# Recurrent chain ranked ahead, spatial maps loaded in the first block, pooling map folded into a weight, pool states by transposes

## The chip, the cores and the metric

One Trainium2 chip, all 8 cores of it; each core runs the same program on its own data, and nothing passes between them. The metric is the device time of one execution, in microseconds, of the slowest core.

## What is computed

Two layers of a hybrid decoder over 8 prompt sequences of 2048 tokens and 128 sample sequences of 8 tokens, width 1024. The reference, cut:

```python
hn = rms_norm(h, norm_mix)
q, k, v, g_out, g_lr, xp, u, vv, gates = split(hn @ w_in)
# A: gated linear attention, 4 heads, d_k 128, d_v 256
g_log = log_sigmoid(g_lr @ w_gk2 + b_gk) / 16
o, s_new = gla_mix(q, k, v, g_log, s_gla)       # S_t = diag(a_t) S_{t-1} + k_t^T v_t, o_t = q_t S_t
branch_a = (rms_norm(o, gla_norm) * silu(g_out)) @ w_br_a
# B: pooling, windows 2/4/8/16, one 128x128 map for each of 4 channel groups
pooled = means - xp
pool_out = einsum('ntgc,gcd->ntgd', pooled, w_mix) * scale
branch_b = pool_out @ w_br_b                    # state: the last 15 rows of [history, xp]
# C: spatial gating in chunks of 128
branch_c = (gelu(u) * (tril(w_s) gelu(vv) + b_s)) @ w_br_c
merged = ga * branch_a + gb * branch_b + gc * branch_c     # ga, gb, gc = sigmoid(gates)
h = h + merged @ w_out
h = h + relu(rms_norm(h, norm_ffn) @ w_ff1)**2 @ w_ff2
```

The outputs are the tokens after a last norm, and the new states of A, B and C. The recurrence starts from zero for a prompt and from a given state (32 pieces of 256 KB a core and layer) for the samples.

## The kernel before

Each core takes one prompt sequence and 16 sample sequences: 17 tiles of 128 tokens, tile 0 being the 16 x 8 sample tokens. The tiles make 5 blocks of 3, 3, 3, 4 and 4 tiles (`BLK`, L24). A product in bf16 covers a block, so its free size is 384 or 512 columns. The normed input of all blocks (`hn`) stays in SBUF for a whole layer.

The main loop (L1100 to L1149) runs, for each layer: the recurrent stage over 5 blocks; the mixing stage over 5 blocks; the gate stage, two halves of the output width over 5 blocks each; the output projection; the feed-forward layers.

*Recurrent stage.* `gla_project` (L744) makes q, k, v and the decays, `gla_gate` (L809) the output gate, `gla_scan` (L838) walks over the prompt tiles with a state `U` and its bf16 copy `Sb` per head. In the scan each tile takes transposes of the keys (`kq` to `ktok`), masked scores (`attT`), the output product, the update of the state on DVE and its copy on ScalarE, and the norm of the output (`o_norm`, L821) with Ln and Exp on ScalarE, where `gla_gate` uses Silu: different function sets of ScalarE, each swap being an ACT_TABLE_LOAD.

*Sample states.* `gla_sample` (L883) is a generator of 32 steps, 8 of which are recorded with each block. A step loads one state into one of five buffers `Sf` (SP's queue), casts it on POOL into one of two `Sinb` (L404), has TensorE multiply the queries with it (`kqS`, `Sinb`) and form the update (`km`, `vS`), updates `Sf` on DVE and writes it out (`gla_s`). The steps are numbered 0 to 31 here; step n uses buffer n mod 5, so its load waits for the write-out of step n - 5.

*Mixing stage.* `mix_block` (L932) projects xp, pools it on DVE into the first half of a block's `OBC`, multiplies each of its 4 channel groups with the pooling map `wpm` and evicts it on ScalarE with the scale, projects u and vv, and applies the spatial map `wsT` (the samples' `wsS`) with the bias. For the new pooling states it projects xp once more, tokens by channels, for the sample tile and the last tile (`proj_tm`). `OBC` is written to HBM and read back in the gate stage as `OBs`; the output of branch A goes the same way as `H4s`.

*Maps.* `mix_prep` (L685) stands after the recurrent stage: it loads the spatial maps in fp32 (`wsp`) on SP's queue and masks them on DVE into `wsT`; an 8 x 8 corner (`w8`) is spread over the 16 samples by a product on TensorE (`rep`).

*Weights.* A ring of 7 slots (`wring`), 2 MB in fp32 each, cast to bf16 on the way, loaded on POOL's queue in a fixed order: v0 v1 k q g0 g1 xp u vv, then for each half ga ba gb bbc gc, and so on (L599 to L616). The slot `bbc` holds half of `w_br_b` and half of `w_br_c`. A load is issued by POOL once the readers of its slot's old content are done.

*What sets the order.* Nothing runs in the order of the code. Every instruction is recorded as a node with a cost (`record`, L199), and `schedule` (L245) places the nodes: per engine it takes the ready node with the least pair of start time and key. The key is the node's number in the code, plus 60 for a node of ScalarE that needs another function set. PSUM tiles are given 8 banks in the same pass. All products are issued at L421, all transposes at L434.

The core of one sample step (L906 to L909):

```python
s = Sf[n % 5]
spq.dma(s.t[:, :, :], sgla[l, i, 2 * hp:2 * hp + 2].rearrange("h d e -> d h e"), writes=[s])
sb_ = Sinb[n % 2]
vcopy(sb_.t[:, :, :], s.t[:, :, :], [s], [sb_], E=POOL)
```

Of the kernel before, what the change touches and what calls it, by code (L numbers as in the profile page):

```python
# [141 lines left out]
class Node:
    __slots__ = ("E", "fn", "reads", "writes", "late", "occ", "lat", "aset", "idx", "succ", "need", "ready", "tiles", "byts")


def build_program():
# [98 lines left out]
    def schedule():  # L245
        free = {id(E): 0.0 for E in (PE, ACT, DVE, SP, POOL)}
        ready = {id(E): [] for E in (PE, ACT, DVE, SP, POOL)}
        bank_at = [0.0] * 8
        bank_of = [None] * 8
        waiting = [n for n in nodes if n.E is PE and any(b.lw is not None for b in n.tiles)]  # L250
        opened = set()
        tiles_in_order = []
# [6 lines left out]
        oldest = 0  # L259
        aset = None  # L260
        dma_at = {id(SP): 0.0, id(POOL): 0.0}
        for n in nodes:
            if n.need == 0:
                ready[id(n.E)].append(n)
        left = len(nodes)
        while left:
            while oldest < len(tiles_in_order) and id(tiles_in_order[oldest]) in opened:
                oldest += 1
            best = None
            for E in (PE, ACT, DVE, SP, POOL):  # L270
                f = free[id(E)]
                pick = None
                for n in ready[id(E)]:
                    s = n.ready if n.ready > f else f
                    key = n.idx
                    bk = None
                    if E is PE and n.tiles and n.tiles[0].k is None:
                        b = n.tiles[0]
                        can = [k for k in b.allowed if bank_of[k] is None]
                        if not can or (len(can) < 2 and b is not tiles_in_order[oldest]):  # L280
                            continue
                        bk = min(can, key=lambda k: bank_at[k])
                        if bank_at[bk] > s:
                            s = bank_at[bk]
                    if E is ACT and n.aset is not None and n.aset != aset:
                        key += 60
                    c = (max(s, f + 30.0), key)
                    if pick is None or c < pick[0]:
                        pick = (c, s, n, bk)
                if pick is not None and (best is None or pick[1] < best[1]):  # L290
                    best = pick
            assert best is not None, "no node can be placed"
            _, s, n, bk = best
            E = n.E
            occ = n.occ
            if E is ACT and n.aset is not None and n.aset != aset:
                occ += 1300.0
                aset = n.aset
            ready[id(E)].remove(n)
            free[id(E)] = s + occ  # L300
            fin = s + occ + n.lat
            if n.byts:
                at0 = max(dma_at[id(E)], s + occ)
                other = dma_at[id(POOL if E is SP else SP)]
                work = n.byts / (310.0 if E is SP else 233.0)
                both = max(0.0, other - at0)
                dma_at[id(E)] = at0 + (both + work - both / 2 if work > both / 2 else work * 2)
                fin = dma_at[id(E)] + 2500.0
            for b in n.tiles:
                if b.k is None:  # L310
                    b.k = bk
                    bank_of[bk] = b
                    opened.add(id(b))
                b.left -= 1
                b.last = max(b.last, fin)
                if b.left == 0:
                    bank_of[b.k] = None
                    bank_at[b.k] = b.last
            rs, ws, lt = real(n.reads), real(n.writes), real(n.late)
            n.fn(rs, ws, lt)  # L320
            for m in n.succ:
                t = fin + (60.0 if m.E is not E or E is not PE else -n.lat)
                if t > m.ready:
                    m.ready = t
                m.need -= 1
                if m.need == 0:
                    ready[id(m.E)].append(m)
            left -= 1
        return max(free.values())
# [132 lines left out]
    r8 = sbc("r8_t", [8, 128])  # L462
# [216 lines left out]
    def mix_consts(l):  # L679
        plq.dma(wpm.t[:, :, :], w_pm[l].rearrange("g c d -> c g d"), writes=[wpm])  # L680
# [251 lines left out]
    def mix_block(l, b):  # L932
# [42 lines left out]
        if b == 0 or b == NB - 1:  # L975
            ps = proj_tm(s, view, b, 0 if b == 0 else nt - 1)
            act(xptok.t[:, :], ps.t[:, :], AF.Copy, [ps], [xptok])
            if b == 0:
                spq.dma(pool_s[l][:, 7:15, :], xptok.t[:, :], reads=[xptok])
            else:  # L980
                spq.dma(pool_p[l], xptok.t[113:128, :], reads=[xptok])
# [236 lines left out]
```

How the kernel before makes its waits and increments, by code:

```python
    def wait(self, tok):  # L41
        if tok is None:
            return
        sem, val = tok
        if sem is self.sem and self.name == "pe":
            return
        k = id(sem)
        if self.seen.get(k, 0) >= val:
            return
        self.e.wait_ge(sem, val)
        self.seen[k] = val
# [1 line left out]
    def tok(self, inst):  # L53
        self.cnt += 1
        inst.then_inc(self.sem, 1)
        return (self.sem, self.cnt)
# [282 lines left out]
            def fn(rs, ws, lt):  # L339
                k = self.i % len(self.sems)
                self.i += 1
                sem = self.sems[k]
                if self.cnt[k] > 0:
                    self.E.wait((sem, 16 * self.cnt[k]))
                acquire(self.E, rs, ws)
                for b in after:
                    self.E.wait(b.w)
                self.E.e.dma_start(out=out, in_=in_).then_inc(sem, 16)
                self.cnt[k] += 1
                release((sem, 16 * self.cnt[k]), rs, ws)
# [283 lines left out]
        def fn(rs, ws, lt):  # L634
            acquire(POOL, rs, ws)
            for view, src in todo:
                nc.gpsimd.dma_start(out=view, in_=src).then_inc(slot_sem[k], 16)
                slot_cnt[k] += 1
            release((slot_sem[k], 16 * slot_cnt[k]), rs, ws)
```

## Time and profile before

| | |
|---|---|
| runs | 3 |
| median | 2469.94 us |
| lowest | 2469.77 us |
| the profiled execution | 2468.97 us |
| its span (core 3, the slowest; the others from 2456.0) | 2467.9 us |
| TensorE (PE) busy | 2379.9 us, 96% of the span |
| VectorE (DVE) busy | 1280.2 us, 52% |
| ScalarE (ACT) busy | 874.9 us, 35% |
| GpSimd (POOL) busy | 125.8 us, 5% |

The profile is of one execution on its slowest core. A busy time is the time in which the engine has an instruction under way; a matmul's end is modelled, and matmuls overlap. PEclk is the clock that was granted to TensorE, as a part of full speed. "x <- y" in a wait says that the instruction which writes x stood still until y was done, and a name such as `OBC` stands for all its buffers. The layers show as two like stretches: the recurrent stage of layer 0 ends near 300 us, that of layer 1 near 1510 us.

### The profile page before, as it was taken

What the parts mean: (1) busy time and instruction counts of PE and PEld (TensorE: products, weight loads), DVE (VectorE), ACT (ScalarE), POOL (GpSimd) and SP (SyncE); (2) the same over time, 40 slices, a digit from 0 to 9 for tenths busy, and PEclk for the clock granted to TensorE, in tenths of its full rate; (3) what the DMA queues carried; (4) which work ended last, traced back from release to release, by engine and by line L of the source; (5) the groups of instructions that cost most, each with busy time, mean ns of one, the idle gap of its engine ahead of it and who ended that gap; (6) DMA issues with size and microseconds to landing.
All of it is one profiled execution on the core that took longest, in us unless ns stands there. A gap on an engine that the chain in (4) does not pass through costs nothing.

```text
span 2467.9 us, 40917 instructions; the slowest of 8 cores (2456.0 to 2467.9 us)
## 1 busy us (share of the span) xinstructions
PE 2379.9 (96%) x13590; PEld 1248.0 (51%) x13590; DVE 1280.2 (52%) x2258; ACT 874.9 (35%) x1803; POOL 125.8 (5%) x179
## 2 busy tenths in 40 slices
PE   6899889999999999999999997999999999999998
PEld 3554445645545444545555554555464454545453
DVE  4776575434456444434656666744343754444455
ACT  4975454222223111212346566532222322111133
POOL 2011100000000000000000110000000000000000
PEclk9999899999999999999999998999999999999999
DMA  9534955236183040405171356562632621322112
GB/s 170 151 92 97 186 174 126 72 69 128 71 169 52 1 69 1 69 1 105 80 133 39 125 96 129 177 129 82 108 94 78 130 50 19 51 35 35 18 61 86
DMA packets 176387, 219.45 MB, mean 89 GB/s; under 512 B 12562, under 2 KB 160538, under 8 KB 173080
## 3 DMA queue, kind: packets, MB, share of 16 engines
q0 software_dynamic: 81168, 78.23, 22.9%
q1 hardware_dynamic: 95016, 138.62, 17.5%
q8 instruction: 115, 1.88, 0.3%
q14 instruction: 88, 0.72, 0.1%
HBM read 240.45 MB, written 55.05 MB: 120 GB/s over the span
## 4 chain that ended last, share of the span: by engine, by line
PE 88%; DVE 3%; DMA 3%; issue 3%; ACT 3%; SPq 0%; POOL 0%; DVEq 0%; ACTq 0%; POOLq 0%
PE ps L421 87%; DMA Sf<-sgla 2%; PE ps L434 1%; DMA wring<-w_in 1%; DVE tmp L395 1%; ACT L384 1%; DMA gla_s<-Sf 0%; ACT rsg L384 0%; DVE Sf L395 0%; ACT Sb L384 0%; ACT sqg L384 0%; DVE xn L395 0%; DVE go L392 0%; DVE U L395 0%; SPq L348 0%
## 5 line engine op out<-in xcount | busy, mean ns | idle before, releaser
L421 PE MATMUL ps<-hn,wring 128*128 128x384 bf16 (+1 forms) x6400 | 1247.0, 348 | 3.1 <-ACT ssq L384 1.1
L421 PEld LDWEIGHTS ps<-hn,wring 128*128 128x128 bf16 x6400 | 624.6, 98 | 545.6 <-issue 9.7
L421 PE MATMUL ps<-wring,a 128*128 128x512 bf16 x2176 | 477.5, 379 | 0.2 <-DVE a L392 0.2
L384 ACT ACTIVATE rl<-ps 128x384 f32<-128x384 f32 (+1 forms) x320 | 170.4, 533 | 644.5 <-PE ps L421 536.3
L392 DVE TENSOR_TENSOR h<-h,ps 128x512 f32<-128x512 f32 x340 | 233.1, 687 | 258.0 <-PE ps L421 255.5
L421 PEld LDWEIGHTS ps<-wring,a 128*128 128x128 bf16 x2176 | 212.5, 98 | 253.2 <-issue 0.7
L392 DVE TENSOR_TENSOR a<-rl 128x384 bf16<-128x384 f32 (+1 forms) x320 | 195.4, 611 | 277.2 <-ACT rl L384 272.0
L384 ACT ACTIVATE sg<-ps 128x384 f32<-128x384 f32 (+1 forms) x240 | 128.0, 533 | 453.7 <-PE ps L421 323.2
L421 PE MATMUL ps<-wring,hn 128*128 128x512 bf16 x848 | 199.8, 384 | 11.5 <-DMA wring<-w_in 8.1
L392 DVE TENSOR_TENSOR tmp<-sg,ps 128x384 f32<-128x384 f32 (+1 forms) x160 | 97.2, 608 | 155.5 <-ACT sg L384 79.8
L421 PE MATMUL ps<-OBs,wring 128*128 128x384 bf16 (+1 forms) x640 | 143.8, 347 | 0.0
L392 DVE TENSOR_TENSOR acc<-sg,ps 128x384 f32<-128x384 f32 (+1 forms) x80 | 48.6, 608 | 173.1 <-PE ps L421 173.1
L421 PEld LDWEIGHTS ps<-wring,hn 128*128 128x128 bf16 x848 | 82.1, 99 | 103.7 <-issue 19.7
L421 PE MATMUL ps<-H4s,wring 128*128 128x384 bf16 (+1 forms) x640 | 130.7, 347 | 0.0
L421 PE MATMUL ps<-wring,mg 128*128 128x512 bf16 x544 | 120.7, 379 | 0.0
L421 PEld LDWEIGHTS ps<-H4s,wring 128*128 128x128 bf16 x640 | 62.6, 98 | 55.0
L421 PEld LDWEIGHTS ps<-OBs,wring 128*128 128x128 bf16 x640 | 62.6, 98 | 55.0
L421 PEld LDWEIGHTS ps<-wring,mg 128*128 128x128 bf16 x544 | 52.5, 98 | 60.0
L637 POOL DMA_DIRECT2D wring<-w_ff x32 | 28.0, 875 | 1063.7 <-PE ps L421 1062.0
L395 DVE SCALAR_TENSOR_TENSOR tmp<-ps,vec_t,rsg 128x256 f32<-128x256 f32 x136 | 63.8, 479 | 30.7 <-ACT rsg L384 27.7
L384 ACT ACT_TABLE_LOAD x51 | 65.4, 1283 | 37.4 <-PE ps L421 30.4
L395 DVE SCALAR_TENSOR_TENSOR Sf<-Sf,eblS,ps 128x256 f32<-128x256 f32 x128 | 58.4, 475 | 20.2 <-PE ps L421 19.4
(137 smaller groups left out, 1788.4 us busy)
## 6 DMA issues: line engine op xcount, KB each, us to landing
wring<-w_ff POOLq DMA_DIRECT2D x32, 1024.0 KB, 14.2
wring<-w_in POOLq DMA_DIRECT2D x30, 1024.0 KB, 15.9
Sf<-sgla SPq DMA_DIRECT2D x64, 256.0 KB, 4.2
gla_s<-Sf SPq DMA_DIRECT2D x64, 256.0 KB, 4.0
H4s<-H_d SPq DMA_DIRECT2D x12, 768.0 KB, 6.7
OBs<-OB_d SPq DMA_DIRECT2D x12, 768.0 KB, 6.2
h_d<-h SPq DMA_DIRECT2D x17, 512.0 KB, 2.6
h<-h_d SPq DMA_DIRECT2D x17, 512.0 KB, 8.1
```

What stands on the lines that cost most here:

```text
L384: op(ACT, lambda: nc.scalar.activation(out=now(out), in_=now(in_), func=func, **kw), reads, writes, occ, 125.0, SETS.get(func))
L392: op(E, lambda: E.e.tensor_tensor(out=now(out), in0=now(in0), in1=now(in1), op=alu), reads, writes, occ, 90.0)
L395: op(DVE, lambda: nc.vector.scalar_tensor_tensor(out=now(out), in0=now(in0), scalar=scalar, in1=now(in1), op0=op0, op1=op1), reads, writes ...
L421: inst = nc.tensor.matmul(now(m[0]), m[1], m[2], start=m[3], stop=m[4], **kw)
L434: inst = nc.tensor.transpose(now(o), i, ident_ap)
L637: nc.gpsimd.dma_start(out=view, in_=src).then_inc(slot_sem[k], 16)
```

## The change

Four edits. The first is in the scheduler: it is written anew as `lay_out(seed)`, and `schedule` takes the best of `ORDERS` layouts, of which there is one. A node's key is now its `rank`, its number less `lift`; `lift` is 200 while `gla_scan` is recorded, 0 elsewhere. A node of ScalarE that needs another function set has 400 ns added to its start in the comparison, besides the 60 on its key. The bookkeeping of nodes, banks and DMA times is otherwise the same.

The second: `mix_prep` and (in layer 0) `mix_consts` are recorded in block 0 of the recurrent stage. The spatial maps are loaded on POOL's queue in bf16 directly into `wsT` and masked in place, and the spread corner `rep` comes from the host; both loads have to follow the load of slot 6 of the ring.

The third: the pooling map is transposed on the host, scaled on DVE, and multiplied into the `w_br_b` half of slot `bbc` at the first block of each half of the gate stage: 4 products of 512 columns, evicted on ScalarE into the slot itself. The products with the pooling map in `mix_block` and their evictions are gone, so `OBC` holds the pooled values.

The fourth: the pooling states come from 4 fp32 transposes of channels already there (`xptok` for the samples, `phist` for the prompt), and the two projections of xp for them are gone.

```diff
@@ constants
+ORDERS = 1
+LIFT = 200
@@ record, lay_out, schedule
+        n.rank = n.idx - lift[0]
...
+        key_of = [n.rank + a for n, a in zip(nodes, (rng.random(len(nodes)) * 4.0 * (seed > 0)).tolist())]
+        swap = 400.0 if seed == 0 else float(rng.integers(0, 1300))
...
+                    c0 = max(s, f + 30.0)
+                    key = key_of[n.idx]
+                    if e == 1 and n.aset is not None and n.aset != aset:
                         key += 60
-                    c = (max(s, f + 30.0), key)
+                        c0 += swap
+                    c = (c0, key)
@@ mix_consts, mix_prep
-        plq.dma(wpm.t[:, :, :], w_pm[l].rearrange("g c d -> c g d"), writes=[wpm])
+        plq.dma(wpm.t[:, :, :], w_pmT[l].rearrange("g d c -> d g c"), writes=[wpm])
+        for g in range(4):
+            ts(wpm.t[:, g, :], wpm.t[:, g, :], vec_t.t[:, V_PSC + l * 4 + g:V_PSC + l * 4 + g + 1], ALU.mult, [wpm, vec_t], [wpm])
...
-        spq.dma(wsp.t[:, :, :], w_spT[l].rearrange("g s t -> s g t"), writes=[wsp], after=[hnB[NTILE - 1]])
-        spq.dma(w8.t[:, :, :], w_spT[l][:, 0:8, 0:8].rearrange("g s t -> s g t"), writes=[w8], after=[hnB[NTILE - 1]])
-        tt(wsT.t[:, :, :], wsp.t[:, :, :], cm.t[:, 0, :].unsqueeze(1).broadcast_to([128, 4, 128]), ALU.mult, [wsp, cm], [wsT])
-        ps = psum()
-        pe_group([(ps.t[:, 0:32], r8.t[:, :], w8.t[:, :, :].rearrange("s g t -> s (g t)"), True, True)], [r8, w8], [ps])
-        act(rep.t[:, :], ps.t[:, 0:32], AF.Copy, [ps], [rep])
+        plq.dma(wsT.t[:, :, :], w_spT[l].rearrange("g s t -> s g t"), writes=[wsT], after=[slots[6]])
+        spq.dma(rep.t[:, :], rep_d[l], writes=[rep], after=[slots[6]])
+        tt(wsT.t[:, :, :], wsT.t[:, :, :], cm.t[:, 0, :].unsqueeze(1).broadcast_to([128, 4, 128]), ALU.mult, [wsT, cm], [wsT])
@@ mix_block
+                act(xptok.t[:, g * 128:(g + 1) * 128], ps.t[:, 0:128], AF.Copy, [ps], [xptok])
...
-        if b == 0 or b == NB - 1:
-            ps = proj_tm(s, view, b, 0 if b == 0 else nt - 1)
+        if b == 0:
+            ps = psum()
+            pe_transposes([(ps.t[:, g * 128:(g + 1) * 128], xptok.t[:, g * 128:(g + 1) * 128]) for g in range(4)], ident.t[:, :], [xptok, ident], [ps])
             act(xptok.t[:, :], ps.t[:, :], AF.Copy, [ps], [xptok])
...
+        if b == NB - 1:
+            ps = psum()
+            pe_transposes([(ps.t[0:15, g * 128:(g + 1) * 128], phist.t[:, g, :]) for g in range(4)], ident.t[:, :], [phist, ident], [ps])
...
-        for g in range(4):
-            ps = psum()
-            pe_group([(ps.t[:, 0:T], wpm.t[:, g, :], ob[:, g, 0:T], True, True)], [wpm, poolB[par][g]], [ps])
-            act(ob[:, g, 0:T], ps.t[:, 0:T], AF.Copy, [ps, vec_t], [poolB[par][g]], scale=vec_t.t[:, V_PSC + l * 4 + g:V_PSC + l * 4 + g + 1])
@@ gate_block
+        if b == 0:
+            for g in range(4):
+                ps = psum()
+                pe_group([(ps.t[:, :], wpm.t[:, g, :], bbc[1][:, g, :], True, True)], [wpm, bbc[0]], [ps])
+                act(bbc[1][:, g, :], ps.t[:, :], AF.Copy, [ps], [bbc[0]])
@@ main loop
+            lift[0] = LIFT
             gla_scan(l, b)
+            lift[0] = 0
             if b == 0:
+                if l == 0:
+                    mix_consts(l)
+                mix_prep(l)
                 samples = gla_sample(l)
...
-        if l == 0:
-            mix_consts(l)
-        mix_prep(l)
```

**Order of TensorE.** The end of layer 0's recurrent stage on TensorE, before. `hn,wring` are products of a projection; `kqS,Sinb` uses a sample state (113 and 114 are the two cast buffers; the first row is step 20, the other one 21); `km` is a state's update; `kq`, `ktok`, `v` and `attT` belong to the scan of the last block, `hst` to the pooling history.

```order
L421 MATMUL ps<-kqS,Sinb_113 128x8 x4
L421 MATMUL ps<-hn,wring 128x512 x8
L421 MATMUL ps<-vS,km_117 128x256 x2
L421 MATMUL ps<-hn,wring 128x512 x64
L421 MATMUL ps<-kqS,Sinb_114 128x8 x4
L421 MATMUL ps<-vS,km_118 128x256 x2
L434 MATMUL ps<-ident_bf,kq_73 128x128 x4
L421 MATMUL ps<-kq_73 128x128 x4
L421 MATMUL ps<-w,r_t 128x32
L434 MATMUL ps<-ident_t,hst 128x120 x4
L434 MATMUL ps<-ident_bf,kq_73 128x128 x4
```

The same place after, from the group behind step 20's product to the one that step 22 follows:

```order
L452 MATMUL ps<-hn,wring 128x512 x8
L452 MATMUL ps<-vS,km_117 128x256 x2
L452 MATMUL ps<-glr,wgk_bf 128x512
L452 MATMUL ps<-hn,wring 128x512 x16
L452 MATMUL ps<-glr,wgk_bf 128x512
L452 MATMUL ps<-hn,wring 128x512 x32
L465 MATMUL ps<-ident_bf,kq_73 128x128 x12
L452 MATMUL ps<-hn,wring 128x512 x8
L452 MATMUL ps<-kq_73 128x128 x4
L452 MATMUL ps<-v_75,ktok_102 128x256 x2
L452 MATMUL ps<-kqS,Sinb_114 128x8 x4
L452 MATMUL ps<-v_75,ktok_102 128x256 x2
```

Between the products of steps 20 and 21 there are 72 projection products before and 64 after, and after them the scan's first transposes and scores stand ahead of step 21 too, with the update of step 20 further forward.

**Order of POOL.** POOL in the same stretch, before: casts of states 17 to 21 (`Sinb<-Sf`), and the issues of weight loads (`wring`: u and vv, then ga0, ba0, gb0) and of layer 1's small gate weights (`wglr`, `wgk`).

```order
L404 CAST Sinb_114<-Sf_110 128x512
L348 DMA wglr<-w_in 128x8x16
L637 DMA wring<-w_in 128x8x512 x2
L404 CAST Sinb_113<-Sf_111 128x512
L404 CAST Sinb_114<-Sf_112 128x512
L348 DMA wgk_bf<-w_gk 16x512 x4
L404 CAST Sinb_113<-Sf_108 128x512
L637 DMA wring<-w_in 128x8x512
L637 DMA wring<-w_br_a 128x8x512
L637 DMA wring<-w_in 128x8x512
L404 CAST Sinb_114<-Sf_109 128x512
L637 DMA wring<-w_br_b 128x4x512
```

After, from the cast of state 18 on; the row ahead of these is the issue of the u weights, and the first `wring` row in it is the issue of the vv weights, then come ga0, ba0 and gb0.

```order
L435 CAST Sinb_113<-Sf_111 128x512
L435 CAST Sinb_114<-Sf_112 128x512
L665 DMA wring<-w_in 128x8x512
L435 CAST Sinb_113<-Sf_108 128x512
L379 DMA wgk_bf<-w_gk 16x512 x4
L665 DMA wring<-w_in 128x8x512
L665 DMA wring<-w_br_a 128x8x512
L435 CAST Sinb_114<-Sf_109 128x512
L435 CAST Sinb_113<-Sf_110 128x512
L435 CAST Sinb_114<-Sf_111 128x512
L435 CAST Sinb_113<-Sf_112 128x512
L665 DMA wring<-w_in 128x8x512
```

The issue of vv has moved from ahead of states 18 and 19 to behind them, and that of gb0, here the last row, from ahead of state 21 to behind state 24.

**Order of TensorE, second place.** Layer 0's gate stage, where the second half begins: `OBs` products are those of the first half's last block, `H4s` products those of the second half's first. Before:

```order
L421 MATMUL ps<-hn,wring 128x512 x8
L421 MATMUL ps<-OBs_131,wring 128x512 x4
L421 MATMUL ps<-hn,wring 128x512 x8
L421 MATMUL ps<-OBs_131,wring 128x512 x4
L421 MATMUL ps<-hn,wring 128x384 x8
L421 MATMUL ps<-H4s_130,wring 128x384 x8
L421 MATMUL ps<-hn,wring 128x384 x8
L421 MATMUL ps<-H4s_130,wring 128x384 x8
```

After, at the same point:

```order
L452 MATMUL ps<-hn,wring 128x512 x8
L452 MATMUL ps<-OBs_130,wring 128x512 x4
L452 MATMUL ps<-wring,wpm_bf 128x512
L452 MATMUL ps<-hn,wring 128x384 x8
L452 MATMUL ps<-wring,wpm_bf 128x512
L452 MATMUL ps<-H4s_129,wring 128x384 x8
L452 MATMUL ps<-wring,wpm_bf 128x512
L452 MATMUL ps<-hn,wring 128x384 x8
L452 MATMUL ps<-wring,wpm_bf 128x512
L452 MATMUL ps<-H4s_129,wring 128x384 x8
```

Four products of the weight slot with the pooling map now stand among the first groups of the half, the first of them directly behind the last product of the block ahead; the numbers behind the names are those of buffers.

## Rows read from the trace of the kernel before

**Rows 1.** The page: its first line, and the chain that ended last, by line

```profile
span 2467.9 us, 40917 instructions; the slowest of 8 cores (2456.0 to 2467.9 us)
...
PE ps L421 87%; DMA Sf<-sgla 2%; PE ps L434 1%; DMA wring<-w_in 1%; DVE tmp L395 1%; ACT L384 1%; DMA gla_s<-Sf 0%; ACT rsg L384 0%; DVE Sf L395 0%; ACT Sb L384 0%; ACT sqg L384 0%; DVE xn L395 0%; DVE go L392 0%; DVE U L395 0%; SPq L348 0%
```

**Rows 2.** Windows: length, busy (count) of PE, PEld, DVE, ACT, POOL; PEclk, DMA share, GB/s

```profile
80.00:140.00 60.00, 51.79 (x431) 32.00 (x430) 52.42 (x96) 53.24 (x124) 2.71 (x4) 1.00 0.42 119
140.00:260.00 120.00, 115.43 (x788) 63.43 (x787) 81.99 (x181) 72.56 (x149) 18.02 (x25) 0.99 0.51 118
260.00:300.00 40.00, 28.65 (x178) 16.97 (x176) 14.00 (x36) 15.35 (x32) 6.30 (x9) 0.83 1.09 179
300.00:352.00 52.00, 45.61 (x324) 26.43 (x322) 43.62 (x111) 34.46 (x70) 4.54 (x7) 0.97 0.52 160
1280.00:1475.00 195.00, 186.99 (x1314) 106.39 (x1313) 126.31 (x280) 124.70 (x268) 16.73 (x23) 1.00 0.31 81
1475.00:1510.00 35.00, 24.95 (x155) 15.12 (x154) 9.85 (x25) 12.28 (x26) 5.41 (x8) 0.80 1.08 185
1510.00:1560.00 50.00, 43.09 (x298) 24.42 (x297) 41.82 (x107) 38.50 (x75) 4.19 (x6) 0.97 0.45 145
```

**Rows 3.** Waits of TensorE, 80 to 350 us: us in total, times, longest

```profile
PE ps L421 <- POOL Sinb L404: 12.6, 6, 8.4
...
PE ps L421 <- DVE OBC L392: 1.1, 2, 0.9
```

**Rows 4.** The same waits, 1280 to 1560 us

```profile
PE ps L421 <- POOL Sinb L404: 10.4, 3, 8.0
...
PE ps L421 <- DVE OBC L392: 2.5, 2, 1.8
```

**Rows 5.** Timeline of TensorE, 259.8 to 284.5 us: start, us, work [idle before <- releaser]

```profile
259.84 13.98 PE L421 MATMUL ps<-hn,wring 128*128 128x512 bf16 x64
282.21 0.25 PE L421 MATMUL ps<-kqS,Sinb 128*128 128x8 bf16 x4 [8.40 <-POOL Sinb L404]
```

**Rows 6.** Timeline of SP's issues, 250 to 275 us

```profile
254.37 7.83 SPq L348 DMA_DIRECT2D gla_s<-Sf  x5
...
263.52 10.87 SPq L348 DMA_DIRECT2D Sf<-sgla  x5
```

**Rows 7.** DMAs issued from 267 to 269 us: count, KB each, us to landing

```profile
Sf<-sgla SPq DMA_DIRECT2D x1, 256.0 KB, 22.7
```

**Rows 8.** The page's DMA issues: count, KB each, median us to landing

```profile
wring<-w_in POOLq DMA_DIRECT2D x30, 1024.0 KB, 15.9
Sf<-sgla SPq DMA_DIRECT2D x64, 256.0 KB, 4.2
```

**Rows 9.** Timeline of TensorE, 407 to 418.4 us

```profile
416.19 1.03 PE L421 MATMUL ps<-OBC,wpm_bf 128*128 128x512 bf16 x4
417.05 1.46 PE L421 MATMUL ps<-hn,wring 128*128 128x384 bf16 x8
```

**Rows 10.** The tile hst: duration in ns, least/median/most

```profile
L434 PE MATMUL ps<-ident_t,hst x16: 407/407/461, 284.3 to 1499.6; 120*128 120x120 f32 x16
```

**Rows 11.** The page's groups: busy us, mean ns | idle before, releaser

```profile
L384 ACT ACT_TABLE_LOAD x51 | 65.4, 1283 | 37.4 <-PE ps L421 30.4
```

**Rows 12.** Timeline of ScalarE, 94 to 120 us

```profile
99.54 1.28 ACT L384 ACT_TABLE_LOAD   x1
100.83 0.49 ACT L384 ACTIVATE go<-ps 128x384 bf16<-128x384 f32 x1
```

**Rows 13.** All waits of the span

```profile
DVE wsT_p L392 <- DMA wsp<-w_spT: 30.7, 2, 15.4
```

**Rows 14.** Timeline of POOL, 540 to 546 us

```profile
544.85 0.75 POOL L637 DMA_DIRECT2D wring<-w_br_c  x1
```

**Rows 15.** DMAs issued from 544.5 to 546 us: count, KB each, us to landing

```profile
wring<-w_br_c POOLq DMA_DIRECT2D x1, 512.0 KB, 18.5
```

**Rows 16.** Timeline of TensorE, 562 to 566 us

```profile
564.12 1.46 PE L421 MATMUL ps<-hn,wring 128*128 128x384 bf16 x8
```

More of the change, by code:

```diff
@@ L137, in __init__ @@
         self.left = 0
-        self.last = 0.0
         self.t = Late(lambda: ps_t[:, self.k or 0, :])
 class Node:
-    __slots__ = ("E", "fn", "reads", "writes", "late", "occ", "lat", "aset", "idx", "succ", "need", "ready", "tiles", "byts")
+    __slots__ = ("E", "fn", "reads", "writes", "late", "occ", "lat", "aset", "idx", "succ", "need", "rank", "tiles", "byts")
 def build_program():
@@ L197, in build_program @@
     nodes = []
+    lift = [0]
     def record(E, fn, reads, writes, occ, lat, late=(), aset=None, byts=0, after=()):
@@ L203, in record @@
         n.idx = len(nodes)
+        n.rank = n.idx - lift[0]
         n.succ = []
-        n.ready = 0.0
         before = {}
@@ L243, in real, with lay_out @@
         return [bank[b.k] if isinstance(b, P) else b for b in bs]
-    def schedule():
-        free = {id(E): 0.0 for E in (PE, ACT, DVE, SP, POOL)}
-        ready = {id(E): [] for E in (PE, ACT, DVE, SP, POOL)}
+    def lay_out(seed):
+        rng = np.random.default_rng(seed)
+        key_of = [n.rank + a for n, a in zip(nodes, (rng.random(len(nodes)) * 4.0 * (seed > 0)).tolist())]
+        swap = 400.0 if seed == 0 else float(rng.integers(0, 1300))
+        engines = (PE, ACT, DVE, SP, POOL)
+        num = {id(E): i for i, E in enumerate(engines)}
+        free = [0.0] * 5
+        ready = [[] for _ in engines]
@@ L248, in schedule @@
         bank_at = [0.0] * 8
         bank_of = [None] * 8
-        waiting = [n for n in nodes if n.E is PE and any(b.lw is not None for b in n.tiles)]
         opened = set()
-        tiles_in_order = []
+        need = [n.need for n in nodes]
+        rdy = [0.0] * len(nodes)
+        kof = {id(b): None for b in tiles_in_order}
+        left = {id(b): b.left for b in tiles_in_order}
+        last = {id(b): 0.0 for b in tiles_in_order}
+        oldest = 0
+        aset = None
+        dma_at = [0.0] * 5
@@ L253, in schedule @@
+        return max(free), order, kof
+    tiles_in_order = []
+    def schedule():
         seen = set()
@@ L258, in schedule @@
                     tiles_in_order.append(b)
[L259 to L286, printed above, removed]
-                    c = (max(s, f + 30.0), key)
[L288 to L328, printed above, removed]
@@ L329, in schedule @@
-        return max(free.values())
+        _, order, kof = min((lay_out(seed) for seed in range(ORDERS)), key=lambda r: r[0])
+        for b in tiles_in_order:
+            b.k = kof[id(b)]
+        for n in order:
+            n.fn(real(n.reads), real(n.writes), real(n.late))
     class DmaQ:
@@ L974, in mix_block @@
         pool_part(xf, 1, Tp, po, b == 0)
-        if b == 0 or b == NB - 1:
-            ps = proj_tm(s, view, b, 0 if b == 0 else nt - 1)
+        if b == 0:
+            ps = psum()
+            pe_transposes([(ps.t[:, g * 128:(g + 1) * 128], xptok.t[:, g * 128:(g + 1) * 128]) for g in range(4)], ident.t[:, :], [xptok, ident], [ps])
             act(xptok.t[:, :], ps.t[:, :], AF.Copy, [ps], [xptok])
[L978 to L981, printed above, removed]
+            spq.dma(pool_s[l][:, 7:15, :], xptok.t[:, :], reads=[xptok])
+        if b == NB - 1:
+            ps = psum()
+            pe_transposes([(ps.t[0:15, g * 128:(g + 1) * 128], phist.t[:, g, :]) for g in range(4)], ident.t[:, :], [phist, ident], [ps])
+            act(xptok.t[0:15, :], ps.t[0:15, :], AF.Copy, [ps], [xptok])
+            spq.dma(pool_p[l], xptok.t[0:15, :], reads=[xptok])
         s, view = wget(l, "u")
```

92 lines of the change are left out of this document (81 added, 11 removed).

## Prediction

> **What bounds the kernel now.** I read the chain of waits first. The line of TensorE from which every product is issued holds 87% of it, and the load of sample states is the largest other piece [rows 1]. So the kernel is bound by TensorE, and an edit gains in two ways: fewer columns streamed, or shorter stretches in which TensorE waits or runs at its lower clock.
>
> Second, the busy time by stretch, to see where such stretches are [rows 2]. All lie where the recurrent stage runs or hands over to the mixing stage. Length less busy time gives the idle TensorE time: 8.2 us in 80:140, 4.6 in 140:260, 11.35 in 260:300, 6.4 in 300:352 for layer 0; 8.0, 10.05 and 6.9 in the three stretches of layer 1; together 55.5 us. The clock adds to it. The granted clock has two levels, 1.2 and 2.4 GHz, so a mean of 0.83 over 40 us is 13.6 us at the lower one, in which up to 6.8 us of work is lost; the same count gives 1.2 in 140:260, 1.6 in 300:352, 7.0 in 1475:1510 and 1.5 in 1510:1560. That is 18.1 us. The ceiling for anything that removes waits is 73.6 us, 3% of the span.
>
> Third, who is waited for. In both layers the first answer is POOL's cast of a sample state: 12.6 and 10.4 us, in single waits of 8.4 and 8.0; the pooling result OBC, which the pooling map reads, comes with 1.1 and 2.5 us [rows 3, 4]. The large wait can be followed: TensorE ends 64 gate products at 273.8 us and then stands 8.40 us for state number 21 [rows 5]. That state is loaded into a buffer whose old content must first be written out. The five write-outs are issued from 254.37 us, the five loads from 263.52 [rows 6], and one of them lands after 22.7 us [rows 7] where 4.2 is usual [rows 8], in a stretch whose 16 DMA engines are full (share 1.09) [rows 2].
>
> **The change, part by part.** The sum is made against the profiled execution's own 2468.97 us: a span of 2467.9 and 1.1 around it. The median of the runs shown is 1.0 us higher.
>
> *TensorE's work.* Four 512-column products take 0.86 us, from 416.19 to the next start at 417.05 [rows 9], 0.215 each. The pooling map goes: 4 groups over 2176 tokens in 2 layers are 17,408 columns, 34 times 512, 7.3 us. The four token-major projections for the pool states go: 32 products, 6.9 us. The fold adds 16 products of 512 columns, 3.4 us. Sixteen fp32 transposes come in. By columns alone (128 of 512) each would be 0.054 us, 0.9 in all; at the whole duration of the nearest row, 0.407, they would be 6.5 [rows 10]. I take 0.2 each, 3.2, since such instructions overlap. Sum: 7.3 + 6.9 - 3.4 - 3.2 = 7.6 us gained, bounds 4.3 and 9.9. All of it lies in stretches where TensorE is the limit, so it counts in full.
>
> *States and the clock behind them* (260:300 and 1475:1510). At stake are 11.35 + 6.8 + 10.05 + 7.0 = 35.2 us. In the new order the last block's scan begins before the gate products, so TensorE asks for states 21 and 22 at once but for 23 to 25 only with scan and gate groups between [order of TensorE]. Against this, state 21 still stands behind eight groups (nine before), and the slots of v0 and v1 come free later: the u weights are issued one row ahead of states 18 and 19 and the vv weights behind them, where both stood ahead before, while gb0 moves behind states 21 to 24 [order of POOL]. The trace has no such order. Bounds: the waits stay (0) or go wholly (35.2), and below nothing in a rival. The nearest row is the wait as it is, so I take a third: 12 us.
>
> *Tail of the recurrent stage* (300:352 and 1510:1560). At stake are 6.4 + 1.6 + 6.9 + 1.5 = 16.4 us. The waits for OBC, 1.1 + 2.5 = 3.6, fall away with their reader. Of the other 12.8 I take a third, 4.4, because the lifted scan of the last block ends earlier against the mixing work: 8.0 us together, bounds 3.6 and 16.4.
>
> *The other scan stretches* (80:260 and 1280:1475). At stake are 8.2 + 4.6 + 1.2 + 8.0 = 22.0 us. Ranking the scan 200 places ahead lets its short products start as soon as they are ready; I take 5 us. It also makes ScalarE swap function sets more often: counting changes of set in its order I get 51 before, as many as the row has loads at 1283 ns [rows 11], and 61 after; ten more are 12.8 us of ScalarE. ScalarE works 53.24 of 60 us in 80:140 [rows 2], so part of that reaches TensorE; I take 3 us. Net 2 us gained, bounds 12.8 lost and 22 gained.
>
> On these loads a page speaks against the change. The trace shows a load of 1.28 us at 99.54 us, and the next activation starts at 100.83, with nothing between [rows 12]. The Trainium skill, page "ScalarE: Activation LUTs", section "What ACT_TABLE_LOAD costs", counts a drain of about 1.38 us besides, 2.66 us a switch; by it the ten would be 26.6 us. This trace shows the load but not the drain, so the row decides.
>
> *Spatial maps.* DVE stood 30.7 us in two waits for their load in the state stretch [rows 13]. I give that nothing of its own: TensorE waited there for the state, which landed later than the map. Loaded early, the map is 256 KB more in the start-up traffic, and in layer 1 POOL and SP wait for the landing of a gate weight ahead of it (a weight takes 15.9 us [rows 8]) while DVE's masking stands in front of the norm copies of the last block. Bounds 0 and 15.9; TensorE then has products of earlier blocks in hand, so I take 2 us lost.
>
> *The fold's wait.* The four fold products stand right behind the last gate product of block 4 [order of TensorE, second place]. For the second half their weights are the slot whose last part is issued at 544.85 us [rows 14] and lands 18.5 us later [rows 15], at 563.3; TensorE reaches that place at 564.12 [rows 16]. Cover is 0.8 us in the kernel before. Queued behind the fold is every later product. Bounds 0 and some 4; I take 1 us lost. The weight's columns are evicted by ScalarE beside the first gate groups.
>
> Sum: 7.6 + 12 + 8 + 2 - 2 - 1 = 26.6 us; 2469.0 - 26.6 = **2442 us**.
>
> **Rivals.** *Only the work counts.* The waits move but keep their sum: 7.6 + 3.6 - 3 = 8.2, giving 2461 us. For it: the transfer that ends last is the same one, behind the same chain of write-out and load. Against it: TensorE gets other work between the states.
>
> *The states land later (slower).* Place: the same wait for state 21 in each layer. Price: with three weight loads beside it the state took 18.5 us more than usual [rows 7, 8], 6.2 a load. The later u and vv loads put one more beside it, 6.2 us of wait, and with the clock's loss (6.8 beside 11.35 idle, a factor of 1.6) 9.9 us a layer, 19.8 in all. Less the 8.2 of the first rival this is 11.6 us slower, 2481 us. It decides from 4.1 us a layer on. Against it: the write-outs start earlier against TensorE's work, since states 16 to 20 stand closer together in the order.
>
> *Function sets on the path.* All ten extra loads delay the chain and the lift gives nothing: the 2 us gained there become 12.8 lost, 14.8 worse than forecast, 2457 us. The drain of the page above would make it 2471.
>
> *Almost every wait goes.* Both state stretches and the tails run through, and half of the other 22: 35.2 + 16.4 + 11 + 7.6 - 3 = 67.2, giving 2402 us. For it: the work that could fill the gaps is in the order. Against it: DMA is full there whatever the order.
>
> **How the numbers follow.** Chances: forecast 0.45 (its own range 2428 to 2455), only the work 0.24, states later 0.13, function sets 0.08, almost every wait 0.10. The range 2416 to 2476 leaves out most of the last and about two thirds of the slower case, under 0.2. About what a measurement of this kernel can tell from no change is 2%, 49 us: faster by more needs 2420 or less, most of the last case and a tail of the forecast, 0.08; slower by more needs 2518, which no case reaches, 0.01; within it 0.91.
>
> **What would show it.** TensorE's work: no product of OBC with the pooling map, 16 of a weight slot with it, busy time lower by about 8 us. States: in the windows around the last block's scan less idle time than 11.35 and 10.05 us and a clock above 0.83 and 0.80; if the wait for POOL's cast is as long as before, that step is wrong. Function sets: 61 loads of 1.28 us. The fold: a wait of TensorE for a weight slot of over 2 us at the start of a half would be a mistake of mine. The forecast as a whole is wrong if the time is above 2461 or below 2420 us.

## The result and the profile after

The changed kernel takes 2438.28 us in the median of four runs (before: 2469.86). The ratio of the two is 0.9868, with a 95% interval from 0.9846 to 0.9891, so it is 1.3% faster, 32.6 us. The profiled execution took 2434.85 us; its slowest core is core 3, as before. Single times named below leave out runs that a loss of clock on a whole die had lengthened (the changed kernel's median is then 2436.74 us), and three runs of the kernel no_lift with a milder loss on two cores, which in the table below raise its ratio (0.993 by the medians without them) and widen its interval.

The page after: the span, and the chain by line, the counterpart of [rows 1].

```profile
span 2433.8 us, 40722 instructions; the slowest of 8 cores (2411.9 to 2433.8 us)
...
PE ps L452 90%; PE ps L465 1%; DMA gla_s<-Sf 1%; DMA Sf<-sgla 1%; DMA wring<-w_in 1%; ACT L415 1%; DMA xt<-xp 1%; ACT rsg L415 0%; DVE xn L426 0%; DVE hx L426 0%; DVE tmp L426 0%; ACT Sb L415 0%; ACT go L415 0%; ACT xj L415 0%; DVE hn L435 0%
```

TensorE's line has gone from 87 to 90% of the chain, and the load of sample states, first among the other pieces before with 2%, now has 1%.

The windows after, cut where the work of [rows 2] now stands (10 us earlier in layer 0, 29 in layer 1); the columns are those of [rows 2].

```profile
80.00:140.00 60.00, 51.61 (x411) 32.78 (x409) 49.64 (x87) 50.01 (x115) 3.84 (x4) 0.91 0.39 115
140.00:250.00 110.00, 105.58 (x758) 59.84 (x757) 79.96 (x180) 74.02 (x148) 13.60 (x20) 1.00 0.46 113
250.00:290.00 40.00, 29.99 (x189) 15.39 (x188) 17.98 (x40) 18.88 (x32) 7.73 (x12) 0.87 1.02 176
290.00:342.00 52.00, 50.30 (x370) 30.66 (x368) 41.05 (x104) 35.71 (x78) 6.04 (x9) 1.00 0.70 185
1251.00:1446.00 195.00, 188.16 (x1346) 108.99 (x1344) 131.62 (x296) 135.21 (x278) 14.31 (x22) 1.00 0.35 86
1446.00:1481.00 35.00, 25.41 (x162) 13.51 (x161) 15.15 (x35) 15.09 (x26) 5.70 (x8) 0.85 0.99 178
1481.00:1531.00 50.00, 48.60 (x354) 29.13 (x353) 37.21 (x96) 35.90 (x78) 5.54 (x8) 1.00 0.68 180
```

Length less busy time, against [rows 2]: the scan stretches 8.4 + 4.4 + 6.8 = 19.6 us (20.8 before), the state stretches 10.0 + 9.6 = 19.6 us (21.4), the tails behind them 1.7 + 1.4 = 3.1 us (13.3). The tails are where the idle time went, and their clock rose from 0.97 to 1.00. Over the whole span TensorE is idle for 75.5 us (2433.8 less 2358.3 busy) where it was 88.0, and busy for 21.6 us less.

The waits of TensorE in the state stretch of layer 0 and of layer 1, after (us in total, times, longest); counterparts of [rows 3] and [rows 4].

```profile
PE ps L452 <- POOL Sinb L435: 10.0, 2, 7.9
```

```profile
PE ps L452 <- POOL Sinb L435: 9.5, 2, 7.2
```

The timeline there, counterpart of [rows 5]:

```profile
262.88 0.38 PE L452 MATMUL ps<-v,ktok 128*128 128x256 bf16 x2
271.19 0.25 PE L452 MATMUL ps<-kqS,Sinb 128*128 128x8 bf16 x4 [7.92 <-POOL Sinb L435]
...
273.93 0.25 PE L452 MATMUL ps<-kqS,Sinb 128*128 128x8 bf16 x4 [2.04 <-POOL Sinb L435]
```

State 21 is waited for 7.92 us (8.40 before) and now 22 for another 2.04. The large wait has stayed on this core.

The page shows the slowest core, and in the changed kernel the cores of one execution differ. The spans go from 2411.9 us (core 4) to 2433.8 (core 3). The waits for the casts are 0.9 to 10.7 us in layer 0 (from 80 to 400 us) and 0.8 to 9.7 in layer 1 (from 1250 to 1600 us). Before, all eight cores had 9.7 to 12.6 and 6.7 to 10.8. The same two rows on core 4, after:

```profile
PE ps L452 <- POOL Sinb L435: 0.9, 2, 0.6
```

```profile
PE ps L452 <- POOL Sinb L435: 1.3, 2, 1.1
```

Which core is slow is not fixed: core 3 took 2433.8 us here, and 2409.3 and 2435.7 in two other executions. The new order can hide the states, then, but on most cores it does not, and the metric is the slowest core.

### The profile page after: what moved, and what is told of

Read it like the earlier page. It is cut to its first block, busy times and chain, and to the rows that moved or that the text cites. A ratio compares the mean times of both kernels' runs of the same rounds, so it can differ in the third digit from the quotient of the medians.

```text
span 2433.8 us, 40722 instructions; the slowest of 8 cores (2411.9 to 2433.8 us)
## 1 busy us (share of the span) xinstructions
PE 2358.3 (97%) x13546; PEld 1239.4 (51%) x13546; DVE 1283.2 (53%) x2266; ACT 874.5 (36%) x1795; POOL 125.7 (5%) x181
## 4 chain that ended last, share of the span: by engine, by line
PE 91%; DMA 4%; ACT 2%; issue 2%; DVE 2%; DVEq 0%; POOL 0%; ACTq 0%; SPq 0%; POOLq 0%
PE ps L452 90%; PE ps L465 1%; DMA gla_s<-Sf 1%; DMA Sf<-sgla 1%; DMA wring<-w_in 1%; ACT L415 1%; DMA xt<-xp 1%; ACT rsg L415 0%; DVE xn L426 0%; DVE hx L426 0%; DVE tmp L426 0%; ACT Sb L415 0%; ACT go L415 0%; ACT xj L415 0%; DVE hn L435 0%
## 5 line engine op out<-in xcount | busy, mean ns | idle before, releaser
L452 PE MATMUL ps<-wring,hn 128*128 128x512 bf16 x816 | 190.2, 382 | 10.4 <-DMA wring<-w_in 8.2
L426 DVE SCALAR_TENSOR_TENSOR U<-U,eblP,ps 128x256 f32<-128x256 f32 x128 | 56.0, 475 | 50.4 <-PE ps L452 49.6
```

The source lines that it names most:

```text
L426: op(DVE, lambda: nc.vector.scalar_tensor_tensor(out=now(out), in0=now(in0), scalar=scalar, in1=now(in1), op0=op0, op1=op1), reads, writes ...
L452: inst = nc.tensor.matmul(now(m[0]), m[1], m[2], start=m[3], stop=m[4], **kw)
```

## The experiments

All were made on the changed kernel, except lift_alone and order_alone, which are made from the kernel before. The column of set loads counts ACT_TABLE_LOAD in the profiled execution.

| kernel | lift | 400 ns | other edits | set loads | ratio to before, 95% interval |
|---|---|---|---|---|---|
| before | no | no | no | 51 | 1 |
| no_lift_swap0 | no | no | yes | 59 | 0.9971 (0.9956 to 0.9986) |
| no_lift | no | yes | yes | 43 | 0.9968 (0.9921 to 1.0014) |
| lift_alone | yes | no | no | 95 | 1.0113 (1.0097 to 1.0129) |
| swap0 | yes | no | yes | 85 | 1.0039 (1.0022 to 1.0056) |
| order_alone | yes | yes | no | 61 | 0.9907 (0.9887 to 0.9926) |
| changed | yes | yes | yes | 61 | 0.9868 (0.9846 to 0.9891) |
| no_fold | yes | yes | no fold | 61 | 0.9885 (0.9849 to 0.9920) |
| proj_states | yes | yes | no transposes | 61 | 0.9877 (0.9825 to 0.9929) |
| late_maps | yes | yes | maps late | 61 | 0.9848 (0.9807 to 0.9889) |
| hold_gates | yes | yes | yes, two loads held | 61 | 0.9822 (0.9806 to 0.9837) |
| hold_vv | yes | yes | yes, three loads held | 57 | 0.9821 (0.9805 to 0.9837) |
| hold_swap800 | yes | 800 | as hold_gates | 53 | 0.9897 (0.9878 to 0.9917) |
| hold_swap1300 | yes | 1300 | as hold_gates | 49 | 0.9903 (0.9886 to 0.9920) |

**One part undone at a time.** First the lift:

```diff
-LIFT = 200
+LIFT = 0
```

> Changed kernel with the lift at 0, all else kept. Theory A (the lift alone lets the scan run beside the mixing work, and with it TensorE's waits and low-clock time after the sample states go): about 18 us of the gain is given back, 2452 to 2460 us against 2437, with TensorE idle again by 5 us or more in the 110 us ahead of each gate stage. Theory B (those waits went because the pooling products and the map work left that stretch): less than 6 us is given back, 2443 us or less, and the stretch ahead of the gate stage keeps under 2.5 us idle.

Four runs took 2451.94 to 2456.13 us, by their median 16 us more than the changed kernel. The 100 us ahead of layer 0's gate stage, on core 0 without the lift and on core 3 with it (windows, columns as in [rows 2]):

```profile
300.00:400.00 100.00, 93.86 (x561) 49.68 (x560) 75.99 (x163) 47.43 (x88) 7.16 (x9) 0.97 0.52 153
```

```profile
300.00:400.00 100.00, 99.44 (x613) 53.54 (x612) 76.41 (x165) 47.48 (x94) 7.18 (x10) 1.00 0.58 161
```

6.1 us idle without the lift, 0.6 with it: theory A, at the lower edge of its range.

Next the fold, undone in code: `mix_block` gets back its four products with `wpm` and their scaled copies, `gate_block` loses the four at b == 0, and the map comes untransposed.

> Changed kernel with the pooling map as 40 products in the mixing stage again, no fold. Theory A: only the work comes back: 40 products that took 8.2 us of TensorE's line in the trace of before less 16 fold products of 3.5 us, 4 to 5 us slower than the changed kernel, about 2442 us. Theory B: the waits for the pooled values come back too, 10 us or more, 2447 us or later.

Four runs gave 2439.95 to 2448.56 us: 4 us above the changed kernel by the ratios, 9 by the medians, with overlapping intervals. That does not tell theory A's 4 to 5 from theory B's 10. The trace speaks for A (what stands behind the second bar is TensorE's idle time before these products):

```profile
L452 PE MATMUL ps<-OBC,wpm_bf 128*128 128x384 bf16 (+1 forms) x40 | 11.8, 347 | 0.6 <-DVE OBC L426 0.5
```

The products are back and TensorE idles 0.6 us before them. The work is what shows; its exact size in time stays open.

The pooling states by projection again:

```diff
-            pe_transposes([(ps.t[:, g * 128:(g + 1) * 128], xptok.t[:, g * 128:(g + 1) * 128]) for g in range(4)], ident.t[:, :], [xptok, ident], [ps])
...
-            pe_transposes([(ps.t[0:15, g * 128:(g + 1) * 128], phist.t[:, g, :]) for g in range(4)], ident.t[:, :], [phist, ident], [ps])
...
+            ps = proj_tm(s, view, b, 0 if b == 0 else nt - 1)
```

> Changed kernel with the pooling states from projections again. Both theories: 32 products of 0.215 us come back (6.9 us), 16 transposes go (2.1 us by their places in the trace): 4 to 6 us slower than the changed kernel, about 2442 us. If ScalarE's extra copies for the transposes had cost as much as the projections, there would be no difference.

2440.96 and 2444.91 us, 2 us more than the changed kernel by the ratios and 6 by the medians, on two runs: in the direction that both theories had, no more can be said. The spatial maps late again, as `mix_prep` of the kernel before has them (`wsp`, `w8` and the product for `rep` come back, and the call stands behind the recurrent stage):

> Changed kernel with the spatial maps loaded after the recurrent stage in fp32 on SP's queue and spread by a product, as before. Theory A (TensorE waits for the states there, not for the maps): 0 to 3 us slower than the changed kernel, 2437 to 2440 us. Theory B (the map load and its masking stood in the way): 6 us or more slower, 2443 us or later, with waits for wsT or for DVE in the stretch behind the states. The prediction gave the early load 2 us lost, by which this would be 2435 us.

2432.41 to 2437.69 us: no slower than the changed kernel (level by the medians, 5 us faster by the ratios, with overlapping intervals). DVE waits for the map again, though for 11.1 us in one wait where it was 30.7 in two [rows 13], in the list of all waits:

```profile
DVE wsT_p L423 <- DMA wsp<-w_spT: 11.1, 1, 11.1
```

This wait is in layer 1 and ends at 1463.39 us. TensorE stands still there for a state, and the cast that releases it begins at 1466.34, after the map. So it was the state that held TensorE up:

```profile
1467.10 0.25 PE L452 MATMUL ps<-kqS,Sinb 128*128 128x8 bf16 x4 [13.38 <-POOL Sinb L435]
```

Loading the maps early is worth nothing that can be measured as a whole, in either direction. It does move idle time. In the 100 us ahead of layer 0's gate stage the kernel with late maps idles 5.3 us on core 2, its slowest, and 5.0 to 6.0 us on the eight cores, where the changed kernel idles 0.1 to 1.0:

```profile
300.00:400.00 100.00, 94.70 (x581) 50.58 (x587) 75.43 (x159) 46.50 (x87) 7.74 (x11) 1.00 0.56 155
```

Against that, from 80 to 140 us its cores run at a mean clock of 0.94 to 1.00, those of the changed kernel at 0.86 to 0.91 (last section).

**What the lift needs.** The lift put on the kernel before by itself:

```diff
-                    key = n.idx
+                    key = n.rank
```

> Kernel before with the rank alone: gla_scan recorded with its key 200 lower, old scheduler, old maps and pooling. Theory A (the parts add up; undoing the lift gave back about 15 us): 13 to 18 us faster than the kernel before, 2452 to 2457 us. Theory B (the lift needs the swap cost or the emptier mixing stage): within 5 us of the kernel before.

Both theories have the wrong time: 27 us slower than before, at 2496.62 us. Theory B's reason, that the lift needs the 400 ns, is borne out by what follows. The changed kernel without the 400 ns:

```diff
-        swap = 400.0 if seed == 0 else float(rng.integers(0, 1300))
+        swap = 0.0
```

> Changed kernel without the 400 ns for another function set in ScalarE's choice (the 60 on the key stays). Theory A (ScalarE's sets are off the path): within 3 us of the changed kernel, 2434 to 2440 us. Theory B (the lifted scan's extra sets are on the path and the 400 ns hold them down): more than 61 loads of 1.28 us and 6 us or more slower, 2443 us or later.

40 us slower than the changed kernel: theory B, far beyond its 6 us. The loads of function sets, with their busy time, mean and idle time before: lift_alone, the kernel without the 400 ns, the changed kernel.

```profile
L387 ACT ACT_TABLE_LOAD x95 | 121.9, 1283 | 38.3 <-PE ps L424 31.3 <-DMA xt<-xs 5.2
```

```profile
L415 ACT ACT_TABLE_LOAD x85 | 109.1, 1283 | 44.4 <-PE ps L452 37.0 <-DMA xt<-xs 6.0
```

```profile
L415 ACT ACT_TABLE_LOAD x61 | 78.3, 1283 | 49.7 <-PE ps L452 42.0
```

The 24 loads more are 30.8 us of ScalarE. Where they strike, in the recurrent stage of layer 1: windows of the kernel without the 400 ns, of the changed kernel in the like stretch, and the waits of the first.

```profile
1280.00:1400.00 120.00, 104.35 (x724) 60.34 (x723) 63.46 (x140) 94.89 (x175) 4.98 (x8) 0.91 0.15 47
```

```profile
1262.00:1382.00 120.00, 115.37 (x860) 69.43 (x859) 75.21 (x169) 86.77 (x185) 6.02 (x10) 1.00 0.20 56
```

```profile
PE ps L452 <- ACT goS L415: 4.1, 2, 3.3
PE ps L452 <- DVE U L426: 3.9, 4, 1.1
PE ps L452 <- DVE tmp L426: 3.4, 3, 2.4
```

15.7 us idle and a clock of 0.91, against 4.6 us and 1.00. TensorE waits for ScalarE's evictions (`goS`) and for DVE behind them. The timeline of ScalarE there shows why:

```profile
1286.80 1.28 ACT L415 ACT_TABLE_LOAD   x1
1288.09 0.38 ACT L415 ACTIVATE go<-ps 128x256 bf16<-128x256 f32 x1
1288.49 1.28 ACT L415 ACT_TABLE_LOAD   x1
1289.79 0.42 ACT L415 ACTIVATE rsg<-rsg 128x256 f32<-128x256 f32 x1
1290.22 1.28 ACT L415 ACT_TABLE_LOAD   x1
1291.52 0.28 ACT L415 ACTIVATE goS<-ps 128x128 bf16<-128x128 f32 x1
```

A lifted node of the scan's norm (`rsg`) takes ScalarE out of the output gate's set (`go`) as soon as it is ready, and the way back is another load: three loads for two activations of 0.4 us. Each load starts at once behind the activation ahead of it and is followed at once by its own, so here too there is no drain of 1.38 us as the Trainium skill counts it (page "ScalarE: Activation LUTs", section "What ACT_TABLE_LOAD costs"). Two more kernels complete the square of lift and 400 ns. The other edits alone (both lines above, LIFT = 0 and swap = 0):

> Changed kernel with the lift at 0 and without the 400 ns, so that only the work, the maps and the pooling states differ from the kernel before. Theory A (the 400 ns only undo what the lift does to ScalarE's function sets): as the kernel without the lift, 2449 to 2456 us. Theory B (the 400 ns are worth something by themselves): only the work is left, 10.6 us by the trace's places, 2457 to 2463 us, with more than the 43 loads of function sets of the kernel without the lift.

2460.4 us in the median of five runs: theory B. The order alone, on the kernel before (the lift and `c0 += 400.0`):

> Kernel before with the lift and the 400 ns, no other edit. Theory A (order and work add up): the changed kernel plus 10.6 us of work, 2445 to 2452 us, with some 60 loads of function sets where the lift alone had 95. Theory B (the order pays only in the emptier mixing stage): 2458 us or later.

2444.03 to 2449.84 us, 2446.46 in the median: theory A. So the other edits are worth 7 us by the ratio, 10 by the medians (2470 to 2460), without the order's edits, and 9.6 with them (0.9907 to 0.9868, and the medians alike). The 400 ns are worth 7 us without the lift (2460 to 2453) and 40 with it; the lift gains 16 us with the 400 ns and loses 16 without (2460 to 2477).

**The wait that stayed.** The loads of ga0 and ba0, which are first used at 400 us, are held until a state has landed:

```diff
+HOLD = 23
+HELD = ('ga0', 'ba0')
...
-        record(POOL, fn, (), [b], 900.0 * len(todo), 0.0, byts=byts)
+        wait_for = [hold[order[n][0][0]]] if order[n][0][1] in HELD else []
+        record(POOL, fn, wait_for, [b], 900.0 * len(todo), 0.0, byts=byts)
...
-                spq.dma(s.t[:, :, :], sgla[l, i, 2 * hp:2 * hp + 2].rearrange("h d e -> d h e"), writes=[s])
+                spq.dma(s.t[:, :, :], sgla[l, i, 2 * hp:2 * hp + 2].rearrange("h d e -> d h e"), writes=[s] + ([hold[l]] if n == HOLD else []))
```

> Changed kernel with the loads of ga0 and ba0 held until sample state 23 has landed. Theory A (the state that TensorE waits 8 us for is late because two weight loads move beside it): the waits for POOL's cast, 10 us a layer in the trace after, fall to 5 us or less in each layer, and the time falls by 8 to 14 us, to 2423 to 2429 us. Theory B (it is late because its buffer's write-out is): the waits stay at 9 us or more and the time within 3 us of 2437. Theory C (held weights come late): a wait of TensorE for a weight slot at the start of the gate stage, and no gain.

2424.46 us, theory A, the fastest kernel here beside the next one. DMAs issued while states 21 to 25 are loaded (count, KB each, us to landing), in the changed kernel and with the two loads held:

```profile
Sf<-sgla SPq DMA_DIRECT2D x5, 256.0 KB, 14.5
wring<-w_in POOLq DMA_DIRECT2D x1, 1024.0 KB, 19.5
wring<-w_br_a POOLq DMA_DIRECT2D x1, 1024.0 KB, 25.7
```

```profile
Sf<-sgla SPq DMA_DIRECT2D x5, 256.0 KB, 5.5
```

(The lists run from 256 to 268 us and from 258 to 268; the held kernel's has no large weight.) A state lands after 5.5 us in place of 14.5 on the slowest core of each kernel, after 4.9 to 7.6 in place of 10.3 to 14.5 on the eight. The Trainium skill says why a load on POOL's queue can slow one on SP's (page "DMA: Bandwidth & Descriptors", section "Issuing engines are not separate DMA queues"): both run on the same 16 engines and interleave; these rows agree. On core 4, the slowest of that execution, the time for which TensorE waits for the casts falls from 10.0 and 9.5 us (core 3 of the changed kernel) to 3.4 and 0.8, in layer 0 and layer 1:

```profile
PE ps L454 <- POOL Sinb L437: 3.4, 2, 3.1
```

```profile
PE ps L454 <- POOL Sinb L437: 0.8, 2, 0.7
```

The cores of the changed kernel show the same without an edit. In layer 0 the issue of ga0 comes 7.2 and 6.5 us behind the first of the five state loads on cores 4 and 5, which wait 0.9 and 1.4 us for the casts; on the six others it comes 2.4 to 4.8 us behind, and they wait 7.3 to 10.7. The start of layer 0's gate stage, where theory C looked, shows no wait. With vv held too (`HELD = ('vv', 'ga0', 'ba0')`):

> The same with the load of vv held too. Theory A: the write-outs ahead of the states have the DMA engines more to themselves, so the waits fall further, to 3 us or less a layer, 2420 to 2427 us. Theory B: as without, 2434 to 2440 us. Theory C: vv now lands too late for its products, and the time is 5 us or more above the kernel with two weights held.

2424.59 us: the waits for casts are nearly gone (1.9 us in the whole span; 0.9 to 1.6 a layer on every core, where up to 4.1 were left), and no time is gained with them. The write-outs land after 6.5 us on core 5, the slowest, where they took 14.1 on the slowest core with two loads held, so late write-outs had a part in the wait too. What the states give back, the tails lose: from 290 to 400 and from 1481 to 1595 us TensorE idles 4.5 and 3.8 us (core 5), where it was 0.6 and 0.8 with two loads held (core 4).

**Fewer loads of sets still.** With 800 and 1300 ns in place of 400 (`swap = 800.0`, `swap = 1300.0`):

> The kernel with ga0 and ba0 held, and 800 ns in place of 400 for another function set. Theory A (ScalarE's sets are still on the path of the scan): about 52 loads in place of 61, 5 to 11 us faster than with 400, 2413 to 2419 us. Theory B (the sets that are left lie beside other work): 2421 to 2428 us.

> The same with 1300 ns, what a load takes in the trace. Theory A: about 48 loads, 6 to 14 us faster than with 400, 2410 to 2418 us. Theory B: no faster than with 400; and if ScalarE now leaves the scan waiting behind work of its present set, 2428 us or later, with more waits of TensorE for rsg and go than the 3.6 and 2.3 us with 400.

Both are 20 us slower than with 400 (2444.54 and 2445.20 us), with 53 and 49 loads: later than both theories for 800, and theory B for 1300. At 800 TensorE idles 15.8 us from 1481 to 1600 us, at a mean clock of 0.91 (core 0), where it is 0.8 us and 1.00 with 400 (core 4). Its waits over the span, at 800:

```profile
PE ps L454 <- ACT sqg L417: 6.9, 5, 5.2
PE ps L454 <- ACT rsg L417: 6.8, 13, 1.0
```

With 400 they are 3.6 us for `rsg` and none for `sqg`. I read this as ScalarE staying in its set while the scan's norm waits; the rest of the 20 us was not separated. Of the values tried 400 ns is the best: a balance between the two, not a cost that is too small.

## Why the prediction was right, and where not

The forecast, 2442 us, is 4 us from the measured median, in part by luck: two of its terms, the states and the tails, were wrong in size and made up for each other.

*TensorE's work* (7.6 us, bounds 4.3 and 9.9): 7 to 10 by the square above, with the maps and the pooling states in it. The parts are as worked out. A fold product takes 0.22 us of the line, as the next start shows. Four transposes take 0.43 us to the next start where other work stands behind them and 0.60 where none does, 2.1 us for all 16 where 3.2 was taken:

```profile
399.57 0.38 PE L452 MATMUL ps<-wring,wpm_bf 128*128 128x512 bf16 x1
399.79 1.46 PE L452 MATMUL ps<-hn,wring 128*128 128x384 bf16 x8
```

```profile
385.30 0.60 PE L465 MATMUL ps<-ident_t,phist 128*15 128x128 f32 x4
385.73 2.54 PE L452 MATMUL ps<-hn,wring 128*128 128x512 bf16 x11
```

*States and the clock behind them* (12 us): wrong for the core that sets the time. On core 3 the waits are nearly as long as before (10.0 and 9.5 us, against 11.4 and 10.0 in the same two stretches); 1.8 us of idle time went, and the clock rose from 0.83 and 0.80 to 0.87 and 0.85. The step had the right suspect, the full DMA engines, and the wrong remedy: the new order leaves ga0 and ba0 in front of the states. hold_gates takes them away and gains 12 us. On the average of the eight cores the step was close: in the two state windows of [rows 2] and their counterparts they idle 18.6 us and run some 22 us at the lower clock before, 11.9 and some 12 after, a gain of 11 us by my estimate, which counts half of the time at the lower clock. The step did not ask how far the cores would spread.

*Tails* (8 us): right in place, too small. 10.2 us of idle time went, and up to 1.6 and 1.5 us of clock loss. In layer 0 it took the lift and the early maps together: without the lift 6.1 us stay idle (no_lift, above), with late maps 5.3 (late_maps, above), and with the lift but with late maps and pooling products 6.1, as the window of order_alone ahead of its gate stage shows (core 4):

```profile
300.00:410.20 110.20, 104.13 (x610) 53.39 (x608) 76.27 (x160) 57.70 (x106) 8.43 (x12) 0.97 0.53 144
```

The pooling products alone do not bring it back: no_fold idles 0.9 to 2.1 us on the eight cores from 300 to 400 us. So most of the 3.6 us that the term took for OBC was not owed to its readers. In layer 1 the order is enough: order_alone idles 1.2 to 2.4 us on the eight cores from 1500 to 1607 us.

*The other scan stretches* (2 us net): idle time fell by 1.2 us, and 10.2 us at the lower clock came in near 113 us (below). The count of 61 loads was right. What failed is that the lift was priced without the 400 ns: as a gain less ten loads, where without them it costs 27 us (lift_alone). The rival of the function sets had the right mechanism, and the edit that I gave no term, the 400 ns, is what keeps it from happening.

*Spatial maps* (2 us lost) and *the fold's wait* (1 us lost): late_maps shows no loss as a whole but a balance, less idle time in layer 0's tail against more time at the lower clock. Nothing waits ahead of the fold: from 400 to 1100 us, where the second half begins too, TensorE waits 0.3 us in all.

Of the 21.6 us of busy time, some 12 to 14 are therefore the same work in less time. In the stretches granted 1.2 GHz TensorE is busy for 31.6 us before and 20.4 after on core 3; at half of the full clock that is 5.6 us of it. The rest was not separated. The mean load of a function set is 1.283 us in every kernel run.

## What to carry to other kernels

Ranking a chain ahead in a list scheduler is only as good as the price it puts on what that chain interrupts: the same lift was worth 16 us or cost 16, by 400 ns in a comparison. When a transfer that the critical engine waits for lands late in a stretch of full DMA engines, look for transfers beside it that are needed much later and hold those. Look at every core: the page of the slowest one showed a wait that two cores of the same execution hardly had. And a sum that comes out right is no proof of its terms: undo the parts one by one, and in pairs where they may need each other.

## What the hardware showed beside this

In the changed kernel all 8 cores run some 10 us at the lower clock near 113 us, which no core of the kernel before does. Windows of the changed kernel, then of the kernel before:

```profile
93.00:103.00 10.00, 7.88 (x64) 5.09 (x63) 8.99 (x15) 8.27 (x16) 0.00 (x0) 1.00 0.75 210
103.00:113.20 10.20, 7.19 (x77) 5.08 (x75) 7.92 (x13) 7.74 (x19) 0.00 (x0) 1.00 0.30 92
113.20:123.40 10.20, 7.68 (x55) 5.08 (x56) 8.14 (x15) 8.21 (x19) 2.16 (x2) 0.50 0.51 151
```

```profile
93.00:103.00 10.00, 8.81 (x65) 5.47 (x64) 7.59 (x13) 8.99 (x17) 0.00 (x0) 1.00 0.61 203
103.00:113.20 10.20, 7.79 (x78) 4.76 (x76) 9.03 (x16) 8.76 (x19) 0.00 (x0) 1.00 0.44 132
113.20:123.40 10.20, 8.05 (x68) 4.56 (x66) 7.09 (x12) 10.14 (x25) 1.16 (x2) 1.00 0.67 149
```

TensorE had been busy for 7.88 of 10 and 7.19 of 10.2 us before the clock fell to 0.50, and for 8.81 and 7.79 in the kernel before, whose clock stayed. What sets the two apart no run here shows. The lift and the early maps both have a part in it: by the mean clock from 80 to 140 us, averaged over the cores, some 12 us are at the lower clock in the changed kernel, 5 with late maps (late_maps), 6 without the lift (no_lift) and none before. Less idle time elsewhere does not protect a kernel from a new thin stretch.
